# Projection units in seven products of quarters, beside a search for thresholds

## The chip, the cores and the metric

One NeuronCore of a Trainium2 chip runs the whole program. The time is the device time of one execution in microseconds; smaller is better. The kernel before was timed three times.

## The reference

The program is one inference step of a one-layer hybrid decoder: 1040 prompt rows (16 learned meta tokens and 1024 tokens) and 8 sequences of 8 new rows, 1104 rows of 1024 in all. Everything is float32. The normalised rows are multiplied by one wide matrix, and its columns are split:

```
h = rms_norm(x, norm1_g) @ w_in
p_r, p_a, g_r, g_a = split_cols(h)          # 1792, 1608, 1024, 1024 columns
y_r, s_fin, shift_last = rwkv7_branch(p_r, shift_prev, s_prev, lp)
q, k, v, qi, wi, ki = dsa_project(p_a, pos)
y_a = attend(q, k, v, qi, wi, ki)
merged = sigmoid(g_r) * (y_r @ w_br_rwkv) + sigmoid(g_a) * (y_a @ w_br_attn)
# in rwkv7_branch: prev = rows one step earlier
pm = p_r + (prev - p_r) * rwkv_mu
# in dsa_prompt, for each block of 128 queries:
score = sum_h relu(qi_h . ki) * wi_h;  keep the 256 highest visible keys;  softmax over them
```

The change touches only how `p_r`, `g_r` and `g_a` are multiplied for the prompt and new rows (the projection units), and when.

## The kernel before

The program runs in stages, each a block of five engine programs which ends when all engines have arrived. The stage of the change is `prompt_and_project` (from 223 to 876 us of the profile). `project_attention` stands before it and has left the normalised rows, turned, in `xT` (8 tiles of 128 channels by 1104 rows). `sample_scores` stands behind it.

`prompt_and_project` does two things at once: the sparse attention of the prompt, and 90 **projection units** that fill TensorE where the attention leaves it free. Unit `u` is tile `t = u // 3` of 128 output channels and column block `j = u % 3` of 368 rows (`COLS`). TensorE's `unit` (L437) is 8 products of 128 x 128 by 368, accumulated in one bank; a float32 product is two instructions in the profile. ScalarE's `evacuate` (L594 to L602) scales the bank into `PMT` and `PX` (tiles 0 to 13) or copies it into `PX` (the gates, tiles 14 to 29). For tiles 0 to 13 GpSimd adds the two (L685, 1040 wide, and L686) and SyncE stores the sum. SyncE loads the weights for two tiles at a time into one of two halves of `W`, as soon as the units of two loads earlier are done.

The stage goes through four parts:

1. The padding (`pad`, L788 to L801, VectorE) and the index products: TensorE `dot` (L453), ScalarE `rectify` (L614), VectorE `weigh` (L719, L721) sum up scores for 83 pieces. After every 20 pieces TensorE does a unit: units 0 to 3. The fifth piece waits for the padding.
2. The **search** (`bisect`): for each query VectorE finds the 256th highest score bit by bit, in 33 rounds. A round is seven counts over the scores (`tally`, L731 and L736, each a pass over up to 1024 columns), TensorE's `total` (L458), which adds up the part that is packed on partitions, a copy of it (L740), and three operations on 128 x 7 numbers (L755, L757, L760). TensorE has a fixed order: twelve product steps, one `total`, and so on (`SPACING` = 12), with units 4 to 58 (`AHEAD` = 59). The products for head team 0 (`scores(0)`) are issued before the search.
3. The choice (`choose`, VectorE), which turns scores into masks; its scan (L775) reads `ones`, set to 1 at the stage's start (L831).
4. 33 **teams** of heads, each two heads after the first. Per head: VectorE `peak_of` (L814), ScalarE `exponential` (L619), VectorE `normalise` (L825, L827), TensorE `tile_up` (L500), ScalarE `untile` (L633), and TensorE `values` (L516). The masks' width m falls from 1040 to 128 columns. `fills(x)` says in which teams a unit is done between these steps, half of it after each `tile_up`: before, in all teams but the last two.

GpSimd moreover issues two gathers of cached index keys (`gather_keys`, L277). The second one writes over `xT`, so it waits for the last projection unit. SyncE's wait for the last store and the drains of all engines end the stage (L366).

## Time and profile before

| | us |
|---|---|
| median of three runs | 2758.52 (2755.36 to 2760.3) |
| the profiled execution | 2736.69 |
| its span | 2734.9 |
| TensorE busy (PE) | 2589.1 (95%) |
| VectorE (DVE) | 1739.7 (64%) |
| ScalarE (ACT) | 788.5 (29%) |
| GpSimd (POOL) | 391.4 (14%) |

PE is the matrix engine's products and PEld its weight loads, which overlap them. Busy shares are means over stages with different limits, so the rows below are from stretches of the one stage. A row of a timeline is: start in us from the span's start, duration in us, engine, line of the program, operation, what it writes and reads, shapes, count, and in brackets how long the engine stood idle before it and what ended that. Several instructions in a row are merged; the duration is then from the first start to the last end. Mean granted clock of TensorE over the span: 0.965.

### The profile page before, as it was taken

Reading aid. Unit: us, or ns where it says so; the run is one execution under the profiler, and the core shown is the slowest. Engines: PE = TensorE matmul, PEld = TensorE weight load, DVE = VectorE, ACT = ScalarE, POOL = GpSimd, SP = SyncE. Lnnn points to the kernel's source line nnn. Section 1 sums busy time; section 2 is a strip of 40 time slices with the busy share of each in tenths; the row PEclk is TensorE's granted clock in tenths of the full one; section 3 lists DMA queues with packets and bytes.
Section 4 is the critical chain, followed back from the end, with each engine's and each line's share of the span. In section 5 each row is a group of like instructions: output and inputs, shape, how many; then the busy total and the mean of one; then the engine's idle time right before and its main releaser. Section 6 shows DMA issues by size and latency. Waiting matters only on the chain.

```text
span 2734.9 us, 49325 instructions
## 1 busy us (share of the span) xinstructions
PE 2589.1 (95%) x19336; PEld 1788.2 (65%) x19336; DVE 1739.7 (64%) x3313; ACT 788.5 (29%) x1725; POOL 391.4 (14%) x574
## 2 busy tenths in 40 slices
PE   8998999999997997898889999998999999999997
PEld 5553566666654323788756997655656666579997
DVE  3555888874533448666668999988762322357666
ACT  2224322124443653111112553012335321221212
POOL 0000111000000000000001663000335441011111
PEclk9999999999998986999999999999999999999999
DMA  8882112131113450000144664443337563533332
GB/s 297 308 292 86 41 64 88 65 103 37 49 41 106 178 162 27 4 27 12 66 146 160 234 241 167 133 122 129 106 133 242 180 201 117 173 124 123 124 124 72
DMA packets 95961, 348.79 MB, mean 128 GB/s; under 512 B 19561, under 2 KB 43977, under 8 KB 74033
## 3 DMA queue, kind: packets, MB, share of 16 engines
q1 hardware_dynamic: 83696, 294.50, 31.3%
q0 software_dynamic: 12032, 51.14, 5.8%
q8 instruction: 153, 2.51, 0.4%
q14 instruction: 80, 0.65, 0.1%
HBM read 289.57 MB, written 55.23 MB: 126 GB/s over the span
## 4 chain that ended last, share of the span: by engine, by line
PE 47%; DVE 7%; DVEq 3%; issue 1%; DMA 1%; POOL 0%; ACT 0%; POOLq 0%; ACTq 0%; SPq 0%
PE banks L2368 6%; PE banks L2281 5%; PE tl_P L2368 4%; PE banks L2313 4%; PE banks L2299 3%; PE tl_P L2313 3%; PE rc_P L1395 3%; PE banks L2213 3%; PE tl_P L2281 2%; DVE arena L2907 2%; DVEq L2905 2%; PE tl_P L2299 2%; DVE tl_v L2901 1%; PE tl_P L2213 1%; PE banks L1407 1%
## 5 line engine op out<-in xcount | busy, mean ns | idle before, releaser
L437 PE MATMUL dp_PS<-base,dp_W 128*128 128x368 f32 x1440 | 465.9, 476 | 0.0
L437 PEld LDWEIGHTS dp_PS<-base,dp_W 128*128 128x128 f32 x1440 | 265.8, 190 | 157.5 <-issue 8.8
L162 PE MATMUL pa_PG<-pa_W,base 128*128 128x402 f32 (+1 forms) x576 | 198.5, 504 | 7.8 <-DMA pa_W<-in_w_dsa 7.7
L736 DVE TENSOR_SCALAR_CACHE_REDUCE dp_EQ<-dp_SCORE,dp_trial 128x1024 f32<-128x1024 f32 (+1 forms) x186 | 176.0, 946 | 19.9 <-issue 0.9
L162 PEld LDWEIGHTS pa_PG<-pa_W,base 128*128 128x128 f32 (+1 forms) x576 | 106.7, 187 | 94.6 <-issue 14.2
L2281 PE MATMUL banks<-base,tl_WU 128*128 128x368 f32 x496 | 157.9, 475 | 0.8 <-DVE base L2960 0.8
L2299 PE MATMUL banks<-base,tl_WD 128*128 128x368 f32 x484 | 154.3, 474 | 0.0
L2901 DVE MAX8 tl_v<-arena 128x8 f32<-128x4100 f32 x32 | 141.8, 4431 | 3.4 <-issue 1.6
L2904 DVE FIND_INDEX8 tl_i<-tl_v,arena 128x8 uint32<-128x4100 f32 x32 | 141.5, 4423 | 0.0
L2907 DVE MATCH_REPLACE8 arena<-tl_v,arena 128x4100 f32<-128x4100 f32 x32 | 141.3, 4414 | 0.0
L2851 POOL DMA_INDIRECT arena<-in_cache_kv,tl_PHT x128 | 122.6, 958 | 109.9 <-PE tl_P L2447 73.8
L2281 PEld LDWEIGHTS banks<-base,tl_WU 128*128 128x128 f32 x496 | 94.0, 191 | 59.5 <-issue 2.8
L2299 PEld LDWEIGHTS banks<-base,tl_WD 128*128 128x128 f32 x484 | 90.5, 190 | 57.1 <-issue 3.7
L2553 ACT ACTIVATE arena<-base 128x368 f32<-128x368 f32 x44 | 22.1, 509 | 270.6 <-DVEq L2944 150.8
L814 DVE CUSTOM_DVE_ANT_0 dp_P<-dp_PS,dp_SCORE 128x1024 f32<-128x1024 f32 (+7 forms) x64 | 48.5, 758 | 66.7 <-PE dp_PS L487 58.8
L2313 PE MATMUL banks<-arena 128*128 128x184 f32 x504 | 85.6, 319 | 1.4 <-DVE arena L3075 1.4
L2225 PE MATMUL banks<-base,arena 128*128 128x368 f32 x256 | 81.3, 473 | 1.5 <-issue 1.1
L2313 PEld LDWEIGHTS banks<-arena 128*128 128x128 f32 x504 | 80.0, 190 | 1.6 <-issue 1.6
L2213 PE MATMUL banks<-arena 128*128 128x368 f32 x240 | 78.5, 480 | 1.1 <-DMA arena<-in_wb 1.1
L2281 PE MATMUL tl_P<-base,tl_WU 128*128 128x368 f32 x240 | 76.8, 473 | 0.0
L2520 POOL TENSOR_TENSOR base<-tl_T 128x368 f32<-128x368 f32 x36 | 30.6, 850 | 302.4 <-ACTq L2603 301.5
L594 ACT ACTIVATE dp_PMT<-dp_PS,dp_rest 128x368 f32<-128x368 f32 x42 | 23.8, 568 | 164.2 <-PE dp_PS L437 164.2
(525 smaller groups left out, 5077.1 us busy)
## 6 DMA issues: line engine op xcount, KB each, us to landing
tl_WU<-in_wu SPq DMA_DIRECT2D x58, 1024.0 KB, 4.9
pa_WQ<-in_wu SPq DMA_DIRECT2D x22, 1024.0 KB, 8.3
wsum<-pa_WS SPq DMA_DIRECT2D x22, 1024.0 KB, 4.9
tl_WD<-in_wd SPq DMA_DIRECT2D x32, 704.0 KB, 4.4
arena<-wsum SPq DMA_DIRECT2D x21, 1024.0 KB, 7.3
dp_W<-in_w_rw SPq DMA_DIRECT2D x15, 1024.0 KB, 5.5
arena<-in_wb SPq DMA_DIRECT2D x24, 512.0 KB, 3.8
arena<-in_wo SPq DMA_DIRECT2D x24, 512.0 KB, 3.8
```

Of the source, the lines that this page charges most:

```text
L162: last = pe.matmul(PG[0:n, c, 0:NC4], xT[:, k, r:r + n], W[:, c, k, :], start=k == 0, stop=k == KD - 1)
L437: last = pe.matmul(bank(f)[:, 0:w], W[:, t // 2 % 2, k, 128 * (t % 2):128 * (t % 2) + 128], xT[:, k, c:c + w], start=k == 0, stop=k == KD - 1)
L736: dve.tensor_scalar(EQ[0:n, 0:m], scored_of(j), values(n, x), None, op, ALU.add, accum_out=result[0:n, x:x + 1])
L2213: last = pe.matmul(out[:, 0:W], WM[:, i % 2, o:o + 128], YT[:, j, k, :], start=k == 0, stop=k == 3)
L2281: last = pe.matmul(out[:, 0:W], WU[:, i % 2, o:o + 128], XN[:, k, :], start=k == 0, stop=k == KD - 1)
L2299: last = pe.matmul(out[:, 0:W], WD[:, i % 3, 128 * e:128 * e + 128], HT[:, f, :], start=f == 0, stop=f == NF - 1)
L2313: last = pe.matmul(out[:, 0:H], weights[:, k, :], moving(k), start=first and k == 0, stop=k == 3, skip_group_check=True)
L2368: last = pe.matmul(out[:, 0:H], weights[:, k, :], moving(k), start=first and k == 0, stop=k == kk - 1, skip_group_check=True)
L2851: pool.indirect_dma_start(out=KV[:, n % 16, t, :], out_offset=None, in_=I["cache_kv"], in_offset=bass.IndirectOffsetOnAxis(ap=PHT[:, 64 * ...
L2901: dve.max(v8[:, :], SC)
L2904: dve.max_index(i8[:, :], v8[:, :], SC)
L2907: dve.match_replace(SC, v8[:, :], SC, TAKEN)
```

## The change

Two things change in `prompt_and_project`.

**Where the units are done.** `fills(x)` becomes true only for x < 27 of the 33 teams, so teams 27 to 30 lose their unit, and `AHEAD` becomes 63: four units more are done between the index products and the teams.

**How units 6 to 59 are done.** These are nine loads of weights (`PAIRS`, q = 1 to 9), each with three column blocks: 27 blocks (`NBL`), each of which makes two units at once, for two tiles of output channels and one column block. A block is a product of a 2 x 2 by a 2 x 2 matrix of quarters: input channels 0 to 511 and 512 to 1023, two output tiles, two halves of 184 rows (`H`). `seven` does it with seven products of quarters (each four TensorE products of 128 x 128 by 184) in place of eight, in banks 0 to 3, with partial results kept by ScalarE (`keep`, seven copies of 184 columns a block) and added by GpSimd (`f16`, `f167`, and three in `finish`). The products take sums of rows (`XF`, made once by `mix_rows` on GpSimd: two column blocks at the stage's start and the third after the index products) and sums of weights (`WF`, four sums of 512 columns for every load, on GpSimd: `weights_a`, `weights_b`, `weights_c`). The results are put together in `STG` in SBUF, from which `evacuate` reads them.

The row mixes of L685 and L686 become `mix_tile` and are called between these sums. `tick` keeps the distance of `total` at twelve steps, a half-width product counting a half. `scores(0)` is issued after the search, since it uses banks 0 to 2. The new tiles lie in the same memory as `RL`, `CUM`, `ones`, `P`, `PTS` and `YB` (one tensor `room_for`); hence `ones` is set after the search, once the evacuations up to unit 59 are done.

The core of the diff; the rest makes the waits and the numbering fit.

```
+    H = COLS[0][1] // 2
...
+        at[0] = 0
+        WF = cut(4 * 512).rearrange("p (i k m) -> p i k m", i=4, k=4)
+        f1, f6, f7, f16, f167 = (cut(H) for _ in range(5))
+        STG = cut(2 * 2 * H).rearrange("p (a n) -> p a n", a=2)
+        XF = cut(3 * 4 * 4 * H).rearrange("p (j i k n) -> p j i k n", j=3, i=4, k=4)
...
-            return int(m >= 256 or x < NTEAM - 2)
+            return int(m >= 256 and x < NTEAM - 6)
         AHEAD = NU - sum(fills(x) for x in range(NTEAM))
         fill_of = [AHEAD + sum(fills(y) for y in range(x)) for x in range(NTEAM)]
         bank = lambda f: PS[:, (4, 6)[f % 2]] if f < AHEAD else PS[:, 7]
+        PAIRS = range(1, AHEAD // 6)
+        BLOCKS = [(q, j) for q in PAIRS for j in range(3)]
+        NBL = len(BLOCKS)
+        by_seven = lambda u: u // 6 in PAIRS
+        nth_product = lambda u: u if u < 6 else u - 2 * NBL
+        nth_copy = lambda u: u // 6 * 6 + 2 * (u % 3) + u // 3 % 2 if by_seven(u) else u
+        FA, FB, FD, FE = (PS[:, x, 0:H] for x in range(4))
+        source = lambda u: STG[:, u // 3 % 2] if by_seven(u) else bank(u)
 
         def scores_of(u):
             m = size(u)[0]
...
                                          xT[:, k, c:c + w], start=k == 0, stop=k == KD - 1)
                     if end == KD:
                         last.then_inc(product, 1)
+
+                def seven(m, tick):
+                    q, j = BLOCKS[m - 1]
+                    c = COLS[j][0]
...
+
+                    def multiply(out, weights, e, moving, first, made):
+                        for k in range(4):
+                            last = pe.matmul(out, weights(e, k), moving(k), start=first and k == 0, stop=k == 3,
+                                             skip_group_check=True)
+                        last.then_inc(made, 1)
+                        tick(2)
+
+                    if j == 0:
+                        pe.wait_ge(w_in[q % 2], 16 * (q // 2 + 1))
+                    pe.wait_ge(fa_taken, 2 * m - 2)
+                    multiply(FA, raw, 0, left, True, fa_made)
+                    pe.wait_ge(xf_made, j + 1)
+                    pe.wait_ge(wf_made, 3 * q - 2)
+                    pe.wait_ge(fb_taken, 2 * m - 2)
+                    multiply(FB, mixed_w, 1, mix(1), True, fb_made)
+                    pe.wait_ge(fd_taken, 2 * m - 2)
+                    multiply(FD, mixed_w, 0, mix(0), True, fd_made)
+                    pe.wait_ge(fa_taken, 2 * m - 1)
+                    multiply(FA, raw, 1, low_left, False, fa_made)
+                    pe.wait_ge(wf_made, 3 * q - 1)
+                    pe.wait_ge(fb_taken, 2 * m - 1)
+                    multiply(FB, mixed_w, 2, mix(2), False, fb_made)
+                    pe.wait_ge(fe_taken, m - 1)
+                    multiply(FE, raw, 3, mix(3), True, fe_made)
+                    pe.wait_ge(wf_made, 3 * q)
+                    pe.wait_ge(fd_taken, 2 * m - 1)
+                    multiply(FD, mixed_w, 3, low_right, False, fd_made)
 
                 def dot(j, p):
...
+                pe.wait_ge(same_in, 16)
+                spent = [0, 0]
+
+                def tick(n):
+                    spent[0] += n
+                    if spent[0] >= SPACING * (spent[1] + 1) and spent[1] < ROUNDS:
+                        total(spent[1])
+                        spent[1] += 1
+
+                for f in range(AMONG, 6):
+                    for k in range(KD):
+                        unit(f, k, k + 1)
+                        tick(1)
+                for m in range(1, NBL + 1):
+                    seven(m, tick)
+                for f in range(6 * PAIRS.stop, AHEAD):
+                    for k in range(KD):
+                        unit(f, k, k + 1)
...
+                pe.wait_ge(fd_taken, 2 * NBL)
+                pe.wait_ge(fe_taken, NBL)
                 scores(0)
-                pe.wait_ge(same_in, 16)
-                steps = [(f, k) for f in range(AMONG, AHEAD) for k in range(KD)]
-                for i, (f, k) in enumerate(steps):
-                    unit(f, k, k + 1)
-                    if i % SPACING == SPACING - 1 and i // SPACING < ROUNDS:
-                        total(i // SPACING)
-                for r in range(len(steps) // SPACING, ROUNDS):
...
                             act.activation(seqs[:, :, 0], sh[:, t], ACT.Copy, scale=mu[:, t:t + 1])
-                    act.wait_ge(product, u + 1)
+                    if by_seven(u):
+                        act.wait_ge(f_done, (u // 6 - 1) * 3 + j + 1)
+                    else:
...
+                def keep(part, bank, made, taken, count):
+                    act.wait_ge(made, count)
+                    act.activation(part, bank, ACT.Copy).then_inc(taken, 1)
+
+                def both(m):
+                    q, j = BLOCKS[m - 1]
+                    act.drain()
+                    evacuate(6 * q + j)
+                    evacuate(6 * q + 3 + j)
+
+                def keep_block(m):
+                    if m > 1:
+                        act.wait_ge(f_mid, m - 1)
+                    else:
+                        act.wait_ge(weighted, len(all_pieces))
+                    keep(f1, FA, fa_made, fa_taken, 2 * m - 1)
+                    keep(f6, FB, fb_made, fb_taken, 2 * m - 1)
+                    if m > 1:
+                        both(m - 1)
+                    keep(STG[:, 1, H:2 * H], FD, fd_made, fd_taken, 2 * m - 1)
+                    keep(STG[:, 0, 0:H], FA, fa_made, fa_taken, 2 * m)
+                    keep(f7, FB, fb_made, fb_taken, 2 * m)
+                    keep(STG[:, 1, 0:H], FE, fe_made, fe_taken, m)
+                    keep(STG[:, 0, H:2 * H], FD, fd_made, fd_taken, 2 * m)
 
                 def rectify(j, p):
...
                     pool.memset(PX[:, i, 0:1], 0.0)
                 pool.drain().then_inc(zeroed, 1)
+
+                def mix_rows(j):
+                    c = COLS[j][0]
+                    high, low, to = xT[:, 0:4, c:c + 2 * H], xT[:, 4:8, c:c + 2 * H], XF[:, j]
+                    pool.tensor_tensor(to[:, 0], high[:, :, H:], high[:, :, 0:H], ALU.subtract)
+                    pool.tensor_tensor(to[:, 2], low[:, :, H:], high[:, :, H:], ALU.subtract)
+                    pool.drain()
+                    pool.tensor_tensor(to[:, 1], low[:, :, H:], to[:, 0], ALU.subtract)
+                    pool.drain()
+                    pool.tensor_tensor(to[:, 3], low[:, :, 0:H], to[:, 1], ALU.subtract)
+                    pool.drain().then_inc(xf_made, 1)
+
...
+                    pool.wait_ge(w_in[q % 2], 16 * (q // 2 + 1))
+                    pool.tensor_tensor(WF[:, 0], part_of(q, 2), part_of(q, 3), ALU.add)
+                    pool.drain()
+                    pool.tensor_tensor(WF[:, 1], WF[:, 0], part_of(q, 0), ALU.subtract)
+                    pool.drain().then_inc(wf_made, 1)
+
+                def weights_b(q):
+                    pool.tensor_tensor(WF[:, 2], part_of(q, 0), part_of(q, 2), ALU.subtract)
+                    pool.drain().then_inc(wf_made, 1)
+
+                def weights_c(q):
+                    pool.tensor_tensor(WF[:, 3], part_of(q, 1), WF[:, 1], ALU.subtract)
+                    pool.drain().then_inc(wf_made, 1)
+
+                def finish(m):
+                    pool.wait_ge(fd_taken, 2 * m)
+                    pool.wait_ge(fe_taken, m)
+                    pool.tensor_tensor(STG[:, 0, H:2 * H], STG[:, 0, H:2 * H], f16, ALU.add)
+                    pool.tensor_tensor(STG[:, 1, H:2 * H], STG[:, 1, H:2 * H], f167, ALU.add)
+                    pool.tensor_tensor(STG[:, 1, 0:H], STG[:, 1, 0:H], f167, ALU.add)
...
-                for t in range(NT):
-                    px, pm = PX[:, t % 2], PMT[:, t % 2]
-                    seqs = px[:, 1 + TP:].rearrange("p (b q) -> p b q", q=9)
-                    later_rows = pm[:, TP:R].rearrange("p (b q) -> p b q", q=8)
...
+                pool.wait_ge(weighted, len(all_pieces))
+                weights_a(PAIRS[0])
+                weights_b(PAIRS[0])
+                weights_c(PAIRS[0])
+                mix_tile(1)
+                mix_rows(2)
+                for m in range(1, NBL + 1):
+                    q, j = BLOCKS[m - 1]
+                    if m > 1:
+                        finish(m - 1)
+                        if j == 0:
+                            weights_c(q)
+                    pool.wait_ge(fa_taken, 2 * m - 1)
+                    pool.wait_ge(fb_taken, 2 * m - 1)
+                    pool.tensor_tensor(f16, f1, f6, ALU.add)
+                    if j == 0 and m > 1 and 2 * q - 2 < NT:
+                        mix_tile(2 * q - 2)
+                    if j == 2 and q + 1 in PAIRS:
+                        pool.wait_ge(fd_made, 2 * m - 1)
+                        weights_a(q + 1)
+                    pool.wait_ge(fb_taken, 2 * m)
+                    pool.tensor_tensor(f167, f1, f7, ALU.add)
+                    pool.drain().then_inc(f_mid, 1)
+                    if j == 0 and m > 1 and 2 * q - 1 < NT:
+                        mix_tile(2 * q - 1)
+                    if j == 2 and q + 1 in PAIRS:
+                        weights_b(q + 1)
+                finish(NBL)
...
-                pool.wait_ge(product, NU)
+                pool.wait_ge(product, NU - 2 * NBL)
...
                 dve.wait_ge(later_in, 16)
-                dve.memset(ones[:, :], 1.0)
                 pad()
...
                 bisect()
+                dve.wait_ge(copied, 6 * PAIRS.stop)
+                dve.memset(ones[:, :], 1.0)
+                dve.drain()
```

## Rows read from the trace of the kernel before

**Rows 1.** Windows: stretch, us, busy us per engine, PEclk, DMA, GB/s.
```profile
304.00:567.00 263.00, 262.80 (x890) 163.03 (x891) 225.57 (x598) 52.13 (x139) 32.11 (x26) 1.00 0.19 69
...
868.00:876.00 8.00, 0.33 (x4) 0.09 (x4) 0.00 (x0) 0.60 (x1) 0.00 (x0) 0.53 0.82 280
876.00:884.00 8.00, 3.41 (x33) 2.93 (x34) 3.14 (x14) 6.54 (x5) 1.02 (x2) 0.50 0.37 78
```

**Rows 2.** Timeline of the search's last rounds, TensorE and VectorE: start, us, engine.
```profile
545.33 0.38 PE L458 MATMUL dp_PS<-dp_part,dp_same 128*128 128x1 f32 x2
...
551.66 0.16 DVE L740 COPY dp_count<-dp_PS 128x1 f32<-128x1 f32 x1
...
559.42 0.16 DVE L740 COPY dp_count<-dp_PS 128x1 f32<-128x1 f32 x1
...
560.97 27.45 PE L437 MATMUL dp_PS<-base,dp_W 128*128 128x368 f32 x88
...
567.29 0.16 DVE L740 COPY dp_over<-dp_PS 128x1 f32<-128x1 f32 x1
```

**Rows 3.** Timeline of the search's entry and first round, VectorE.
```profile
305.86 0.92 DVE L844 COPY base<-base 64x128 f32<-64x128 f32 x4
...
307.36 0.29 DVE L731 TENSOR_SCALAR_CACHE_REDUCE dp_EQ<-dp_PACK 128x130 f32<-128x130 f32 x1
...
315.63 0.16 DVE L740 COPY dp_count<-dp_PS 128x1 f32<-128x1 f32 x1 [1.99 <-PE dp_PS L458]
```

**Rows 4.** Timeline of TensorE in a later stage: two blocks of seven half-width products.
```profile
1525.80 1.49 PE L2313 MATMUL tl_P<-base,tl_WU 128*128 128x184 f32 x8
...
1534.60 1.41 PE L2313 MATMUL tl_P<-base,tl_WU 128*128 128x184 f32 x8
```

**Rows 5.** Groups by form, GpSimd: line, op, tiles, shapes, count, busy, mean ns.
```profile
L685 POOL TENSOR_TENSOR dp_PMT<-dp_PMT,dp_PX 128x1040 f32<-128x1040 f32 x14 | 31.0, 2217 | 211.3 <-ACTq L603 211.3
...
L2801 POOL TENSOR_TENSOR base<-arena 128x184 f32<-128x184 f32 x21 | 12.1, 576 | 0.0
...
L2030 POOL TENSOR_TENSOR arena<-tl_WU 128x512 f32<-128x512 f32 x1 | 1.3, 1265 | 117.2 <-DMA tl_WU<-in_wu 117.2
```

**Rows 6.** Timeline and one line's instructions: VectorE beside a GpSimd instruction.
```profile
503.06 2.03 POOL L685 TENSOR_TENSOR dp_PMT<-dp_PMT,dp_PX 128x1040 f32<-128x1040 f32 x1 [12.62 <-ACTq L603]
503.13 1.98 DVE L755 TENSOR_SCALAR dp_step<-dp_count 128x7 int32<-128x7 f32 x1
...
1540.87 0.45 DVE L2908 COPY arena<-tl_v 128x8 f32<-128x8 f32 x1
...
L755 DVE TENSOR_SCALAR dp_step<-dp_count x31: 170/171/1983, 323.5 to 559.7; 128x7 int32<-128x7 f32 x31
...
L731 DVE TENSOR_SCALAR_CACHE_REDUCE dp_EQ<-dp_PACK,dp_trial x31: 348/348/351, 316.4 to 552.6; 128x130 f32<-128x130 f32 x31
```

**Rows 7.** Timeline of the stage's start: GpSimd, VectorE, TensorE.
```profile
223.68 0.13 POOL L675 MEMSET dp_PX<- 128x1 f32 x2 [38.49 <-POOLq L37]
...
230.01 0.93 DVE L831 MEMSET dp_ones<- 128x1040 f32 x1 [7.32 <-DMA dp_later<-in_later]
...
232.92 0.28 PE L536 MATMUL dp_PS<-ident,dp_WD 16*128 16x16 f32 x1 [5.68 <-DVEq L805]
```

**Rows 8.** Timeline of the last teams, TensorE and VectorE.
```profile
836.96 0.66 PE L516 MATMUL dp_PS<-dp_PTS,V 128*64 128x128 f32 x8
...
866.31 0.44 PE L516 MATMUL dp_PS<-dp_PTS,V 128*64 128x128 f32 x4 [1.91 <-ACTq L637]
...
861.04 0.29 DVE L814 CUSTOM_DVE_ANT_0 dp_P<-dp_PS,dp_SCORE 128x128 f32<-128x128 f32 x1 [4.02 <-PE dp_PS L487]
...
863.26 0.29 DVE L827 TENSOR_SCALAR dp_P<-dp_P,dp_den 128x128 f32<-128x128 f32 x1
```

**Rows 9.** Instructions of L366, the end of the stage's block: min/median/max ns, start.
```profile
L366 POOLq DRAIN  x1: 11388/11388/11388, 863.7 to 863.7; - x1
...
L366 SPq DRAIN  x1: 7/7/7, 870.0 to 870.0; - x1
```

More of the change, by code:

```diff
@@ L369, in load @@
                 def load(p):
-                    if p >= 2:
-                        sp.wait_ge(product, 6 * (p - 1))
+                    if p - 2 in PAIRS:
+                        sp.wait_ge(fd_made, 6 * (p - 2))
+                    elif p >= 2:
+                        sp.wait_ge(product, nth_product(6 * (p - 2)) + 6)
                     sp.dma_start(W[:, p % 2], I["w_rw"][:, p]).then_inc(w_in[p % 2], 16)
@@ L378, in sends @@
                     if j == 2 and t >= NT:
[L379 removed]
+                        sp.wait_ge(copied, nth_copy(u) + 1)
                         sp.dma_start(gates[t - NT], PX[:, t % 2, 0:R]).then_inc(gate_out[t % 2], 16)
@@ L433, in unit @@
                     if first == 0 and f >= 2:
-                        pe.wait_ge(copied, f - 1 if f < AHEAD else f)
+                        past = f if f >= AHEAD else f - 1 if not by_seven(f - 2) else 6
+                        pe.wait_ge(copied, past)
                     c, w = COLS[j]
@@ L542, in _ @@
                 pe.wait_ge(rectified, len(all_pieces))
[L543 to L551 removed]
+                pe.wait_ge(same_in, 16)
[14 more added lines that the diff above has]
+                        unit(f, k, k + 1)
+                        tick(1)
+                for r in range(spent[1], ROUNDS):
+                    total(r)
+                pe.wait_ge(fa_taken, 2 * NBL)
+                pe.wait_ge(fb_taken, 2 * NBL)
+                pe.wait_ge(fd_taken, 2 * NBL)
+                pe.wait_ge(fe_taken, NBL)
+                scores(0)
                 pe.wait_ge(copied, AHEAD)
@@ L654, in _ @@
                         evacuate(d // EVERY)
-                for f in range(AMONG, AHEAD):
+                for f in range(AMONG, 6):
+                    evacuate(f)
+                for m in range(1, NBL + 1):
+                    keep_block(m)
+                both(NBL)
+                for f in range(6 * PAIRS.stop, AHEAD):
                     evacuate(f)
@@ new lines, in weights_c @@
+                def weights_c(q):
[7 more added lines that the diff above has]
+                    pool.tensor_tensor(STG[:, 1, 0:H], STG[:, 1, 0:H], f167, ALU.add)
+                    pool.drain().then_inc(f_done, 1)
@@ new lines, in mix_tile @@
+                def mix_tile(t):
+                    px, pm = PX[:, t % 2], PMT[:, t % 2]
+                    seqs = px[:, 1 + TP:].rearrange("p (b q) -> p b q", q=9)
+                    later_rows = pm[:, TP:R].rearrange("p (b q) -> p b q", q=8)
+                    pool.wait_ge(copied, nth_copy(3 * t + 2) + 1)
+                    pool.tensor_tensor(pm[:, 0:TP], pm[:, 0:TP], px[:, 0:TP], ALU.add)
+                    pool.tensor_tensor(later_rows, later_rows, seqs[:, :, 0:8], ALU.add)
+                    pool.drain().then_inc(mixed, 1)
@@ L677, in _ @@
+                mix_rows(0)
+                mix_rows(1)
                 pool.wait_ge(weighted, dots0[0] + len(pieces(0)) + 1)
@@ L679, in _ @@
                     pool.dma_start(PACK[16 * x:16 * x + 16, :], SCORE[0:16, PW16 * x:PW16 * x + PW16]).then_inc(packed, 16)
-                for t in range(NT):
-                    px, pm = PX[:, t % 2], PMT[:, t % 2]
-                    seqs = px[:, 1 + TP:].rearrange("p (b q) -> p b q", q=9)
-                    later_rows = pm[:, TP:R].rearrange("p (b q) -> p b q", q=8)
-                    pool.wait_ge(copied, 3 * t + 3)
-                    pool.tensor_tensor(pm[:, 0:TP], pm[:, 0:TP], px[:, 0:TP], ALU.add)
-                    pool.tensor_tensor(later_rows, later_rows, seqs[:, :, 0:8], ALU.add)
-                    pool.drain().then_inc(mixed, 1)
+                mix_tile(0)
+                pool.wait_ge(weighted, len(all_pieces))
[4 more added lines that the diff above has]
+                mix_rows(2)
+                for m in range(1, NBL + 1):
+                    q, j = BLOCKS[m - 1]
[19 more added lines that the diff above has]
+                finish(NBL)
                 pool.wait_ge(masked, 1)
```

35 lines of the change are left out of this document (25 added, 10 removed).

## Prediction

> **What bounds the kernel now.** I read the windows first, to find which engines are full in the stage that changes. In the search (304 to 567 us) TensorE is busy for 262.8 of 263 us and VectorE for 225.6, GpSimd for 32.1 [rows 1]. A full TensorE suggests that cheaper products would pay, so the next view is the timeline of one round. One round's `count` is read at 551.66 and the next one's at 559.42: 7.76 us, with VectorE waiting for nothing, while TensorE's twelve product steps (24 instructions, at 27.45/88 = 0.312 us each) take 7.49 us [rows 2]. The search has two full engines; VectorE sets its end (567.29), and TensorE's 88 leftover instructions (27.45 us) run beside the choices that follow [rows 2]. The teams of heads after it are bound by TensorE as long as a unit of products is filled into each. At the end of the block SyncE is ready at 870.0, but GpSimd's drain, which began at 863.7, lasts 11.39 us [rows 9], and 8 us pass with TensorE empty [rows 1].
>
> **TensorE in the search.** Before: 55 units of 8 products; 88 instructions are 5.5 units, so 5.0 us a unit, 275 us. After: units 4 and 5 and 60 to 62, 25 us, and 27 blocks of seven half-width products. Such a block takes 8.80 us in the later stage (1525.80 to 1534.60) [rows 4] instead of two units' 10.0, so 27 blocks are 238 us. Together 263 us: TensorE does four units more in 12 us less. But as VectorE sets the end, those 12 us are worth nothing; what counts is what the sums on GpSimd do to VectorE.
>
> **GpSimd beside VectorE.** L755, a 128x7 operation on VectorE, starts at 503.13, just after GpSimd's L685 (503.06, 2.03 us), and takes 1.98 us where the middle one of 31 takes 0.17; a 128x8 copy in a later stage takes 0.45 us in the same way. The tallies do not mind: all 31 of L731 take 348 to 351 ns [rows 6]. Each round has three such small operations (L755, L757, L760) between its last tally and the next. GpSimd's instructions are 0.58 us (184 wide), 1.27 (512) and 2.22 (1040) [rows 5]. In the search it will have 27 x 5 of 184, 9 x 4 of 512, four of 736 (between 512 and 1040: about 1.6 us, an estimate), and 13 row mixes of 1040 (2.22, and 0.3 allowed for L686): 78 + 46 + 6 + 33 = 163 us of some 285, busy 57%. An operation that arrives at random waits on average the sum of the squared durations over twice the time: (135 x 0.33 + 36 x 1.61 + 4 x 2.6 + 13 x 4.9) / 570 = 0.31 us. The second and third come 0.25 us later; GpSimd's instructions stand mostly in rows of two or three, so the next one has often begun: 0.2 us each. That is 0.7 us a round and 22 us in 32 rounds, less the 1.8 us that L755 lost before: **+20.6 us**. Bounds: only one wait a round, +8; three waits of about 0.45, +40.
>
> The Trainium skill (SBUF — State Buffer, section "Who interferes with whom") says that whoever issues first holds the shared port pair for its whole instruction while the other fully blocks, and that on VectorE this concerns two-port modes and two inputs from SBUF. The row for L755 agrees (1.98 us against 0.17). By that rule all three small operations are exposed, which gives the 20.6; by the row alone only L755 is, which gives the lower bound of +8.
>
> **The start of the stage.** Eight 736-wide sums (`mix_rows` 0 and 1) now start on GpSimd at 223.7 and last until about 236.6. VectorE's padding had its 0.93 us memset of `ones` at 230.01 [rows 7] and then six small copies and a sum (L793 to L801). The memset leaves (-0.9), but each of those seven operations now lets one GpSimd instruction pass, so the padding ends at about 238, not 232.9, when TensorE had waited 5.68 us for it [rows 7]. TensorE is nearly full from there to the search, so all passes on: **+5.0** (bounds -0.9, if copies slip in between, and +6).
>
> **Entry of the search.** GpSimd's first four weight sums (4 x 1.27 = 5.1 us) start as VectorE does its last causal add, the index, four copies of L844 and one more before its first tally at 307.36 [rows 3]: **+3.8** (+1.3 to +5.3). The first tally waited 1.99 us for TensorE [rows 3] behind `scores(0)`, which is moved behind the search: **-1.9**. The memset comes back between search and choice, with drain **+1.0**; its wait for 60 evacuations is met by then, since the last block ends a round before. `scores(0)` and the three leftover units (13.7 us) are done before VectorE's three choices are.
>
> **TensorE's clock.** TensorE then has nothing to do for about 12 us until the first peak. After the 8 us with no product the granted clock was 0.50 for the next 8 us [rows 1]. At 1.2 instead of 2.4 GHz the first full microseconds cost about half of themselves: **+2.5** (0 to +5).
>
> **Last teams.** From the values of team 26 to those of team 31 it took 836.96 to 866.31 = 29.35 us [rows 8], four of the five intervals holding a unit of 5.0. Without it VectorE's own work is 861.04 to 863.55 = 2.5 us, and its 4.02 us wait for score products held a half unit of 2.5, so 1.5 remains [rows 8]: 4.0 us a team, four of them and the 2.7 of the last: 18.7, so -10.6. As TensorE is then under half busy its clock may fall here too, +1.6: **-9** (-15 to -5).
>
> **End of the block.** The second gather waits for the last product, which now comes about 18 us before the end of the block instead of 5; the drain's 11.4 us fit in. SyncE's 870.0 then sets it, not 875.1 [rows 9]: **-5** (0 to -5).
>
> Every step's waits in `seven` have cover: the sums of block m-1 (1.75 us), ScalarE's two evacuations (about 2.5 us) and one copy end before the seventh product of block m, 7.5 us in; if that cover goes, each microsecond is paid 27 times. SyncE's weight load still waits for the block two ahead; the row mixes' DMAs come at most 2 us later.
>
> **Sum.** +5.0 + 3.8 - 1.9 + 20.6 + 1.0 + 2.5 - 9 - 5 = **+17 us**. The profiled execution took 2736.69 us (span 2734.9), so 2754; the median of the timed runs is 2758.52, 22 us above, and the prediction goes with it: 2775.5 us.
>
> **Rivals.** (A) The forecast, VectorE slowed by GpSimd, chance 0.55.
> (B) Faster: the small operations rarely meet a GpSimd instruction, because GpSimd's instructions follow TensorE's products in a fixed order while the tallies' ends fall in between. Then -1.9 - 0.9 + 1 + 2.5 - 9 - 5 = -13 us: 2745. For it: in the whole search only one of 31 L755 was caught, with GpSimd busy 12%. Against: 57% busy, and a block has 14 steps and a round 12, so their phases drift through all positions. It decides when a round loses less than 0.15 us. Chance 0.16.
> (C) One wait a round (+8 for +20.6) and the padding untouched: about -1 to +4, 2760. Chance 0.12.
> (D) GpSimd itself becomes the bound: waits for VectorE and ScalarE stretch its chain beyond 9.5 us a block, TensorE waits in `seven`, and the tallies come late. At 10.5 us a block 27 blocks take 284 us, and three waits a round, together +35 to +40: 2796. For it: 6 us of GpSimd a block and in a block with two row mixes 9. Against: no row shows it falling behind. Chance 0.17.
>
> **Range and chances.** 0.2% is 5.5 us, about what a measurement of this kernel can tell from none. Slower by more: A and D and a little of C, 0.74; within: the rest of C, 0.10; faster: B, 0.16. The range takes in B's near end and nearly all of D: 2745 to 2796; A's own is 2763 to 2790.
>
> **What would show it.** The distance of L740's copies: 8.3 to 8.7 us (7.76 kills A, and 9.5 or more speaks for D). L755, L757 and L760 with durations above 0.2 us, each ending with a GpSimd instruction. TensorE's wait for `padded` ending near 238. Last interval of values 4.0 us instead of 6.7. L366's drain on GpSimd over before SyncE's, and the next stage 1 us after it. If TensorE waits for `xf_made`, `wf_made` or a `taken` inside the blocks by more than 1 us each, the chain that I took as covered was not.

## The result and the profile after

The changed kernel took 2765.12 us (median of 11 runs, 2757.44 to 2770.13) against 2755.36 for the kernel before (11 runs): ratio 1.0031, 95% interval [1.0017, 1.0045]. By this ratio it is slower by 8.5 us (the two medians lie 9.8 us apart); the forecast was +17. The time lies inside the forecast's range of 2745 to 2796 us, but only half of the forecast change came.

The first comparison of profiles misleads. The profiled execution of before took 2736.69 us, less than each of its timed runs (2751 and more); the one of the changed kernel took 2757.44. Cut at the ends of the stages, the 20 us do not stand where the code differs. The last of the rows below is SyncE's release at the end of the stage of the change, the counterpart of 875.3 before (870.0 plus the rest of GpSimd's drain [rows 9]); L389 is L366 before.

```profile
L389 POOLq DRAIN  x1: 10546/10546/10546, 857.1 to 857.1; - x1
...
L389 SPq DRAIN  x1: 7/7/7, 878.6 to 878.6; - x1
...
L389 SPq EVENT_SEMAPHORE  x1: 17/17/17, 878.8 to 878.8; - x1
```

The stage ends 3.5 us later than before. Three stages on, at 1395.5 (before 1396.0), even that is gone in this pair of profiles; the last stage, whose code is the same, takes 1358.9 us instead of 1337.7. TensorE's timeline of the changed kernel there shows where:

```profile
2070.67 0.77 PE L2466 MATMUL banks<-base,tl_WU 128*128 128x368 f32 x1 [2.33 <-issue]
2073.47 0.77 PE L2466 MATMUL banks<-base,tl_WU 128*128 128x368 f32 x1 [2.03 <-issue]
2076.27 0.77 PE L2466 MATMUL banks<-base,tl_WU 128*128 128x368 f32 x1 [2.03 <-issue]
```

One product, then 2 us in which TensorE waits for nothing that the profile shows, again and again, while GpSimd issues its gathers. The experiments start with this stretch, since a price of 20 us would have hidden all others.

The windows of the changed kernel, for the same length of the search, for the choices behind it, and for the first team's start (columns as in [rows 1]):

```profile
322.00:585.00 263.00, 253.32 (x1579) 245.22 (x1577) 229.67 (x574) 113.19 (x326) 152.99 (x197) 0.99 0.23 75
594.00:609.00 15.00, 2.72 (x12) 1.44 (x10) 13.66 (x15) 0.16 (x1) 5.35 (x9) 0.66 0.78 214
609.00:617.00 8.00, 7.73 (x27) 4.01 (x28) 3.70 (x8) 2.56 (x5) 0.00 (x0) 0.78 0.00 0
```

GpSimd is busy for 153 us of 263 instead of 32, TensorE for 253 instead of 263: its twelve product steps are over before VectorE's round is. The three small operations of a round, the read of the total, and the tallies (lines' instructions; min/median/max in ns):

```profile
L938 DVE TENSOR_SCALAR dp_step<-dp_count x31: 170/173/1495, 329.5 to 577.7; 128x7 int32<-128x7 f32 x31
L940 DVE TENSOR_TENSOR dp_bits<-dp_bits,dp_step x31: 166/167/529, 329.9 to 577.9; 128x7 int32<-128x7 int32 x31
L943 DVE TENSOR_SCALAR dp_trial<-dp_bits x30: 170/171/1882, 330.1 to 570.4; 128x7 int32<-128x7 int32 x30
L923 DVE COPY dp_count<-dp_PS x32: 157/159/160, 321.6 to 577.4; 128x1 f32<-128x1 f32 x32
L919 DVE TENSOR_SCALAR_CACHE_REDUCE dp_EQ<-dp_SCORE,dp_trial x186: 612/946/1281, 323.0 to 576.7; 128x1024 f32<-128x1024 f32 x31, 128x896 f32<-128x896 f32 x31, 128x768 f32<-128x768 f32 x31, 128x640 f32<-128x640 f32 x31
```

The medians are untouched. A stretched operation starts inside a GpSimd instruction and ends 0.02 to 0.03 us after one; the longest, on VectorE and GpSimd:

```profile
386.65 1.88 DVE L943 TENSOR_SCALAR dp_trial<-dp_bits 128x7 int32<-128x7 int32 x1
386.48 2.02 POOL L833 TENSOR_TENSOR dp_PMT<-dp_PMT,dp_PX 128x1040 f32<-128x1040 f32 x1 [0.18 <-issue]
```

Of the 92 small operations 30 last longer than 0.2 us: 5.4, 2.4 and 6.4 us too much for the three lines. 31 rounds take 255.8 us (321.6 to 577.4; before 243.8 [rows 2, 3]). Start of the stage and entry of the search, VectorE and TensorE:

```profile
229.68 3.36 DVE L976 COPY dp_QZ<-QT 64x32 f32<-64x32 f32 x4
233.35 1.59 DVE L983 COPY dp_QIZ<-base 64x64 f32<-64x64 f32 x2
234.96 1.75 DVE L984 TENSOR_TENSOR dp_WD<-ident,WI 16x128 f32<-16x128 f32 x1
...
309.23 1.40 DVE L884 SCALAR_TENSOR_TENSOR dp_SCORE<-dp_later,dp_SCORE 128x128 f32<-128x128 f32 x1
310.71 1.21 DVE L1022 TENSOR_SCALAR idx<-pt,base 128x8 int32<-128x8 int32 x1
311.83 1.89 DVE L1026 COPY base<-base 64x128 f32<-64x128 f32 x4
313.74 1.17 DVE L1028 COPY base<-KIT 128x64 f32<-128x64 f32 x1
...
315.27 0.29 DVE L914 TENSOR_SCALAR_CACHE_REDUCE dp_EQ<-dp_PACK 128x130 f32<-128x130 f32 x1
```

```profile
236.79 0.28 PE L600 MATMUL dp_PS<-ident,dp_WD 16*128 16x16 f32 x1 [9.63 <-DVEq L988]
...
608.95 3.72 PE L551 MATMUL dp_PS<-base,QT 64*128 64x512 f32 x8 [12.28 <-DVEq L1002]
...
856.98 0.66 PE L580 MATMUL dp_PS<-dp_room_for,V 128*64 128x128 f32 x8
...
874.25 0.70 PE L580 MATMUL dp_PS<-dp_room_for,V 128*64 128x128 f32 x4 [0.45 <-ACTq L746]
```

The padding ends at 236.8 instead of 232.9 [rows 7], the first tally starts at 315.3 instead of 307.4 [rows 3], and TensorE stands idle for 12.28 us before the second team's scores. The last two rows answer to 836.96 and 866.31 of [rows 8]: 17.3 us instead of 29.35.

### The profile page after: what moved, and what is told of

Read it like the earlier page. It is cut to its first block, busy times and chain, and to the rows that moved or that the text cites. A ratio compares the mean times of both kernels' runs of the same rounds, so it can differ in the third digit from the quotient of the medians.

```text
span 2755.6 us, 51292 instructions
## 1 busy us (share of the span) xinstructions
PE 2571.3 (93%) x19984; PEld 1862.5 (68%) x19984; DVE 1761.6 (64%) x3313; ACT 849.2 (31%) x1914; POOL 531.9 (19%) x757
## 4 chain that ended last, share of the span: by engine, by line
PE 47%; DVE 7%; DVEq 3%; issue 1%; another core or an unknown queue 1%; DMA 1%; ACT 0%; POOL 0%; ACTq 0%; SPq 0%; POOLq 0%
PE banks L2553 6%; PE banks L2466 5%; PE tl_P L2553 4%; PE banks L2498 4%; PE banks L2484 3%; PE tl_P L2498 3%; PE tl_P L2466 3%; PE banks L2398 3%; PE rc_P L1580 2%; DVE arena L3092 2%; DVE tl_v L3086 2%; DVEq L3090 2%; PE tl_P L2484 2%; PE tl_P L2398 1%; PE banks L1592 1%
## 5 line engine op out<-in xcount | busy, mean ns | idle before, releaser
L463 PE MATMUL dp_PS<-base,dp_W 128*128 128x368 f32 x576 | 190.0, 476 | 1.0 <-ACT dp_room_for L723 1.0
L162 PEld LDWEIGHTS pa_PG<-pa_W,base 128*128 128x128 f32 (+1 forms) x576 | 106.7, 187 | 94.5 <-issue 14.2
L463 PEld LDWEIGHTS dp_PS<-base,dp_W 128*128 128x128 f32 x576 | 104.7, 190 | 64.6 <-issue 8.8
L480 PE MATMUL dp_PS<-dp_room_for 128*128 128x184 f32 x648 | 111.7, 321 | 0.0
L480 PEld LDWEIGHTS dp_PS<-dp_room_for 128*128 128x128 f32 x648 | 102.4, 190 | 0.0
L691 ACT ACTIVATE dp_room_for<-dp_PS 128x184 f32<-128x184 f32 x189 | 57.5, 324 | 126.5 <-PE dp_PS L480 120.7
L997 DVE CUSTOM_DVE_ANT_0 dp_room_for<-dp_PS,dp_SCORE 128x1024 f32<-128x1024 f32 (+7 forms) x64 | 48.5, 758 | 57.7 <-PE dp_PS L551 50.3
```

The lines of the kernel that those rows point to most:

```text
L162: last = pe.matmul(PG[0:n, c, 0:NC4], xT[:, k, r:r + n], W[:, c, k, :], start=k == 0, stop=k == KD - 1)
L463: last = pe.matmul(bank(f)[:, 0:w], W[:, t // 2 % 2, k, 128 * (t % 2):128 * (t % 2) + 128], xT[:, k, c:c + w], start=k == 0, stop=k == KD - 1)
L480: last = pe.matmul(out, weights(e, k), moving(k), start=first and k == 0, stop=k == 3, skip_group_check=True)
```

## The experiments

In the expectations T1 is what I took for true, R (R1, R2, R3) a rival. Each kernel was timed beside the kernel before on the same chip, in four groups. In them before took 2755, 2736, 2756 and 2735 us (the last two groups carry the same chip number); so ratios are given, and the ends of the stage, which did not depend on that.

**A second profile of each kernel** (b0: before; a0: changed; no edit).

> The kernel before, unchanged, for a second profile. In the profiles at hand the stage of the change ends 3.5 us later after the change (875.3 to 878.8), the stage behind the two next ones takes it back (312.9 to 309.0 us), and the whole difference of 20.7 us stands in the last stage (1337.7 to 1358.9 us), whose code is the same: between 2063 and 2087 TensorE waits about 2.03 us ahead of one product after another, put down to issue. T1: this stretch is chance (the first profile of before was an execution without it, 2736.7 us against 2751 to 2762 in eleven timed ones): then this profile has it too, in an execution of 2750 to 2762 us with 1350 to 1360 us in the last stage. R1: the stretch belongs to the changed kernel: then the last stage is 1338 +- 3 here again and the execution about 2737.

> The changed kernel, unchanged, for a second profile. All theories: the stage of the change ends at 878.8 +- 1.5, the mean round of the search is 8.2 to 8.3 us. T1: the last stage differs from its 1358.9 by up to 20 us either way. R1: it is 1359 +- 3.

b0 took 2753.97 us, and its last stage 1358.5; a0 2757.47, with 1357.3. TensorE's rows of the kernel before (b0) in the same place:

```profile
2069.42 0.77 PE L2281 MATMUL banks<-base,tl_WU 128*128 128x368 f32 x1 [1.33 <-issue]
2072.22 0.77 PE L2281 MATMUL banks<-base,tl_WU 128*128 128x368 f32 x1 [2.03 <-issue]
2075.02 0.77 PE L2281 MATMUL banks<-base,tl_WU 128*128 128x368 f32 x1 [2.03 <-issue]
```

R1 falls: the stretch belongs to neither kernel. In all profiles of my runs beside which before took 2755 us the last stage lasts 1357 to 1361 us, beside 2736 us 1333 to 1341, whatever the kernel; only the first profile of before (1337.7, beside timed runs of 2755) doesn't fit this. Stage ends: before 875.3 and 874.3, changed 878.8 and 879.4. The stage costs 3.5 to 5.1 us, not 17. Three stages on, this second pair still stands 4.7 us apart (1392.4 and 1397.1), so that the difference was gone there in the first pair was chance.

**Half of the change each** (fills_only: before with the new `fills`; seven_only: changed with the old).

```
-            return int(m >= 256 or x < NTEAM - 2)      # before -> fills_only
+            return int(m >= 256 and x < NTEAM - 6)     # after -> seven_only: the reverse
```

> The kernel before with fills(x) as in the change (four units moved from teams 27 to 30 to before the teams) and all else left. T1 (the terms of the prediction): the rounds stay 7.86 us on average, the four units follow the search on a full TensorE (+20), the last teams give back 9 to 10.6, and the drain at the end of the block is hidden (-5): stage end at 880 to 882, time +4 to +7 us, ratio about 1.002. R2: the last teams are bound by TensorE without their unit too: then it gives all 20 back, and the stage ends at 870 to 872.

> The changed kernel with fills(x) of before (units in all but the last two teams, AHEAD = 59; 24 blocks of seven instead of 27, units 54 to 58 by eight products). T1: the start (+5 to 6) and the rounds (mean 8.2 to 8.3 us) are as in the changed kernel, the last teams take 6.7 us each again (+9 to +10), and GpSimd's drain at the end of the block is late again (+5): stage end 892 to 895, 14 to 16 us later than the changed kernel, ratio to before about 1.007. R2 (it is the fills that cost, and seven products are free): stage end at 875 +- 2.

fills_only: stage end 875.4, ratio 1.0013 [1.0001, 1.0025]. seven_only: stage end 896.3, ratio 1.0068 [1.0049, 1.0088]. R2 falls both times. T1 was 5 us too high for fills_only: the first team came 18 us later and the last teams gave 13 back, not 10. It was 1 us too low for seven_only. Without seven products the four units cost 1 us in the profile and 3.6 us in the timed runs; beside seven products they are worth 17 us (896.3 against 879; seven_only also has 24 blocks of seven instead of 27, since `AHEAD` is 59). They fill idle time: in seven_only TensorE waits twice as long before the second team's scores (its waits: us in total, times, longest), and the stage ends 4.4 us after SyncE's drain, with GpSimd's.

```profile
PE dp_PS L551 <- DVEq L1002: 24.3, 1, 24.3
```

**Row sums after the padding** (late_rows).

```
+                pool.wait_ge(padded, 1)
                 mix_rows(0)
                 mix_rows(1)
```

> The changed kernel, but GpSimd waits for VectorE's padding before the row sums of the first two column blocks. T1 (the small copies of the padding queue behind GpSimd's 736-wide sums): TensorE's wait for the padding is 5.0 us again (9.5 in the changed kernel), and the stage ends 4 us earlier, at 874.5 to 876; GpSimd's sums now meet the weighting of the first pieces, which costs 1 us or none. R2: they set that chain back by as much as they did the padding: stage end 878.5 to 880.

T1 and R2 both had the sign wrong: stage end 888.0, ratio 1.0036 [1.0024, 1.0048]. The padding is as quick as before (0.54 us for the four copies that took 3.36), but the weighting is not. Timelines of VectorE and GpSimd:

```profile
230.21 0.54 DVE L977 COPY dp_QZ<-QT 64x32 f32<-64x32 f32 x4
...
234.01 8.46 DVE L905 SCALAR_TENSOR_TENSOR dp_SCORE<-dp_room_for,WI,dp_SCORE 128x512 f32<-128x512 f32 x4
242.88 6.03 DVE L905 SCALAR_TENSOR_TENSOR dp_SCORE<-dp_room_for,WI,dp_SCORE 128x512 f32<-128x512 f32 x3
```

```profile
241.88 2.20 POOL L796 TENSOR_TENSOR dp_room_for<-base 128x736 f32<-128x736 f32 x1
244.22 2.00 POOL L798 TENSOR_TENSOR dp_room_for<-base,dp_room_for 128x736 f32<-128x736 f32 x1
```

VectorE's back-to-back sums of two SBUF inputs take turns with GpSimd's, 2.1 us each instead of 0.84 (3.36 for four in a0): 8.6 us lost in these seven. Beside that TensorE does 26 instructions from 240 to 260 where it did 61 in a0, at a granted clock of 0.57 (a0: 0.99), and VectorE then waits 7.9 us for TensorE's L531 where it waited 3.65 in a0; what of this is the clock's share no run separates. The padding was the cheaper victim.

**Two more units ahead** (more_ahead: `x < NTEAM - 8`), **numbers of the search in PSUM** (psum_state), and these with late_rows (combined).

```
+                    count, b_ps = PS[:, 7, 0:NS], PS[:, 7, 8:8 + NS].bitcast(I32)   # psum_state
-                        dve.tensor_tensor(bits[:, :], bits[:, :], step[:, :], ALU.bitwise_xor)
+                        dve.tensor_tensor(b_ps if b else bits[:, :], b_ps, step[:, :], ALU.bitwise_xor)
...
+                            dve.tensor_scalar(trial[:, :], b_ps, 1 << (b - 1), None, ALU.bitwise_xor)
```

> The changed kernel with two units more moved ahead of the teams (fills for x < NTEAM - 8, AHEAD = 65; still 27 blocks of seven). TensorE stands idle for 12.3 us before the first peak of the changed kernel, and two units are 10 us. T1: the peak comes at the same time (+-0.5 us), teams 25 and 26 take 2.2 to 2.7 us less each, and the idle time that lowered TensorE's clock is gone (-0.5 to -1): stage end at 873 to 875. R2 (more of the last teams are bound by a chain of VectorE and ScalarE, which the unit only fills): stage end 878 to 879.

> The changed kernel with count and bits of the search held in a bank of PSUM, so that each of the three small operations of a round has an input from PSUM instead of SBUF. In the changed kernel 28 to 33 of the 92 last longer than 0.2 us, 14.2 and 15.1 us in all (two profiles). T1 (they wait for GpSimd at a port of SBUF that a source in PSUM does not need): none of them is above 0.35 us, the rounds lose at most 0.1 us each for access to PSUM, mean 7.80 to 7.95 instead of 8.23, stage end 866 to 871, unless TensorE's blocks now set the rounds, for which 7.6 us each is enough. R3 (it is any access to SBUF, or the output, that waits): a third or so still stretched, mean round above 8.15.

> All three edits together: row sums after the padding, two more units ahead, count and bits in PSUM. T1: their gains add up, except that the search now ends 12 us earlier relative to TensorE, so the two units and the three leftover ones (24 us) are no longer hidden in full behind the choices: 4 + 12 + 5 less 2 to 4. Stage end at 860 to 864, 11 to 15 us before the kernel before, ratio 0.994 to 0.997. If the parts overlap (R): ratio 0.999 to 1.001.

more_ahead: stage end 876.7, ratio 1.0001 [0.9992, 1.0010], 2 us later than T1. The teams give 5.5 us back as expected; the rounds happened to lose 17.6 us to GpSimd instead of 14 to 15, which took half of it. psum_state: 876.9, 1.0006 [0.9996, 1.0016]. Its lines:

```profile
L939 DVE TENSOR_SCALAR dp_step<-dp_PS x31: 165/165/166, 330.8 to 575.7; 128x7 int32<-128x7 f32 x31
L941 DVE TENSOR_TENSOR dp_PS<-dp_PS,dp_step x30: 173/174/174, 331.0 to 567.8; 128x7 int32<-128x7 int32 x30
L944 DVE TENSOR_SCALAR dp_trial<-dp_PS x30: 166/166/167, 331.3 to 568.1; 128x7 int32<-128x7 int32 x30
L919 DVE DVE_READ_ACCUMULATOR dp_EQ<-dp_SCORE,dp_trial x186: 140/142/144, 325.1 to 575.2; 128x1 f32 x186
```

This is the cleanest evidence for the mechanism: with one input in PSUM no small operation is stretched by a nanosecond, beside the same sums on GpSimd. Most of the gain was lost again, since the six accumulators a round that are now read into PSUM take 0.142 instead of 0.083 us, 11 us in 32 rounds; the median round is 8.12 us, and T1's stage end (866 to 871) was missed. combined: 879.1, 1.0013 [1.0004, 1.0022], neither T1 nor R; late_rows' loss of 9 us goes through it and takes what the two others gave.

**Only what is needed** (bits_only: `bits` in PSUM, `count` in SBUF; weights_later; two_edits: both; three_edits: `mix_rows(1)` moved as well; "mean round" is over 32 rounds).

```
-                pool.wait_ge(weighted, len(all_pieces))    # weights_later
+                pool.wait_ge(indexed, 1)
                 weights_a(PAIRS[0])
...
-                mix_tile(1)                                # three_edits; out of the stage's start
+                mix_rows(1)
+                mix_tile(1)
```

> The changed kernel with only bits in PSUM. With count and bits there no small operation was stretched, but each of the seven READ_ACCUMULATOR of a round took 0.14 instead of 0.08 us and the mean round was 8.13. T1 (an operation that reads or writes two things in SBUF at the double rate, or reads two, waits for GpSimd): L938's successor (count to step, both in SBUF) is still stretched in a third of the rounds, 4 to 6 us in all, the two others never; mean round 7.90 to 8.00, stage end at 869 to 872 against 879. R3 (only the accumulators' detour held the small operations out of GpSimd's way in time): the two others are stretched again, mean round above 8.1.

> The changed kernel, but GpSimd's first four weight sums wait for VectorE's index and query copies (indexed) instead of the last weighting. T1: the operations ahead of the search (1.39, 1.21, 1.89 and 1.16 us in the changed kernel, 0.29, 0.23, 0.92 and 0.19 before) are as before, the first tally starts 4 us earlier (311.2 against 315.2), TensorE still finds the sums made at its first block; stage end 875 to 876. R2: the sums come too late and TensorE's first block and so the rounds start 2 to 4 us later: stage end 878 to 879.

> The two edits together (bits in PSUM, first weight sums after the copies). T1: the search ends 12 to 14 us earlier than in the changed kernel; TensorE then has no idle time before the first peak, and its own work (594 to 597 us until the scores of the first team) begins to set it: stage end 866 to 869, 6 to 9 us before the kernel before (874.3, 875.3), ratio 0.997 +- 0.0015. If the gain is lost to TensorE altogether: stage end 873 or later, ratio 1.000.

> The same, and the row sums of the second column block moved from the stage's start to behind the first weight sums. T1: the padding meets at most one GpSimd sum more (230 to 231 us), TensorE's wait for it is 6 to 7 us instead of 9.5, 2.5 to 3.5 us gained at the first tally; of these 1 to 2 are lost where the sums for the second block come late. Stage end 864 to 868. R: GpSimd's queue in the first three blocks gets so long (it now carries 14 us of row sums there) that TensorE waits 5 us or more: stage end 870 or later, later than two_edits.

| | first count | mean round | lost in small operations | stage end | ratio |
|---|---|---|---|---|---|
| bits_only | 321.9 | 7.97 | 5.6 | 870.5 | 0.9990 [0.9982, 0.9999] |
| weights_later | 318.3 | 8.41 | 20.1 | 881.2 | 1.0025 [1.0015, 1.0034] |
| two_edits | 318.1 | 8.05 | 8.4 | 869.6 | 0.9980 [0.9966, 0.9994] |
| three_edits | 312.9 | 8.22 | 7.4 | 869.9 | 0.9982 [0.9972, 0.9992] |

bits_only, two of its three lines:

```profile
L939 DVE TENSOR_SCALAR dp_step<-dp_count x31: 170/171/1260, 329.7 to 569.6; 128x7 int32<-128x7 f32 x31
L944 DVE TENSOR_SCALAR dp_trial<-dp_PS x30: 165/166/167, 330.4 to 562.3; 128x7 int32<-128x7 int32 x30
```

T1 holds to the line: the operation with both ends in SBUF is still caught, the one with a source in PSUM is not. weights_later removes the 1.40, 1.21, 1.89 and 1.17 us (VectorE's first tally at 311.95 instead of 315.27) and is not faster than the changed kernel by its stage end (881.2): shifted by 3 us, the rounds lose 20.1 instead of 15 to the same GpSimd sums, met at other places. Both T1 and R2 were too early here. With `bits` out of reach (two_edits) most of that lottery is gone, but not the part of `count`. The search ends 9 to 10 us earlier than in the changed kernel, not 12 to 14, and my guess that TensorE would then set the start of the teams was wrong: it still waits 12.3 us before the scores. In three_edits the rival came true by its cause: GpSimd has all row sums of the second and third column block to do before the first sum of block 1 (`f16`, at 329.47); ScalarE waits 7.8 us for it, TensorE 4.7 us for ScalarE, and VectorE for TensorE's total, twice, 6.6 us in all. The longer of the two:

```profile
340.61 0.16 DVE L923 COPY dp_count<-dp_PS 128x1 f32<-128x1 f32 x1 [4.01 <-PE dp_PS L522]
```

**Controls and the best version.** before_bits is the kernel before with bits_only's edit, two_ahead and three_ahead are two_edits and three_edits with `x < NTEAM - 8`, after_again is the changed kernel.

> The kernel BEFORE with bits of the search in PSUM. GpSimd is nearly idle there (13% busy in the search), so by T1 the edit finds nothing to save but the one stretched operation (1.65 to 1.8 us): mean round 7.80 to 7.86, stage end 872.5 to 875, ratio 0.9995 to 1.0000. If the 0.999 of bits_only comes from a cheaper round as such (R), the rounds here are shorter than 7.76 in the median and the ratio is 0.997.

> two_edits with two units more ahead of the teams (x < NTEAM - 8). two_edits still shows TensorE idle for 12.3 us before the first peak. T1: the peak is not moved, teams 24 and 25 give 5.4 us back: stage end 864 +- 1, ratio 0.996 to 0.997. R: TensorE's two units end behind the peak: stage end 867 or later, ratio 0.998.

> three_edits with the same two units more ahead. TensorE's idle time before the first peak was 10.3 us there. T1: stage end 864 to 865. R: 868 or later. Against two_ahead: no difference that can be told, since three_edits and two_edits differed by 0.3 us in stage end.

> The changed kernel again, timed beside the others of this call. Two profiles ended its stage 4 to 5 us later than before (878.8 and 879.4; 875.3 and 874.3), the timed runs gave +8.5 us [1.0017, 1.0045]. T1: stage end 879 +- 1 in this profile too, ratio 1.001 to 1.003, as the stage alone gives 0.0018; if it is 1.003 or more again, timed runs lose 3 us or more outside of what the profiles show.

before_bits: stage end 874.4, ratio 1.0003 [0.9994, 1.0012]. The edit is worth nothing that can be told where GpSimd is nearly idle (its one stretched operation, from `count`, stays), so the 8 to 9 us that it gains in bits_only are those of the contention. two_ahead: stage end 864.2, ratio 0.9966 [0.9954, 0.9978], faster than both kernels by a third of a per cent and more; TensorE's wait before the scores has shrunk as it should:

```profile
570.53 23.74 PE L463 MATMUL dp_PS<-base,dp_W 128*128 128x368 f32 x76
594.11 3.95 PE L542 MATMUL dp_PS<-base,dp_QZ 128*128 128x512 f32 x12
600.43 2.55 PE L551 MATMUL dp_PS<-base,QT 64*128 64x512 f32 x8 [2.37 <-DVEq L1003]
```

three_ahead: 863.8, 0.9972 [0.9963, 0.9981], as good. after_again: stage end 880.0, ratio 1.0032 [1.0021, 1.0042].

## Why the prediction was wrong

The direction and the mechanism held, the size was off by half: +17 us forecast, +8.5 measured. The step that failed is the term for GpSimd beside VectorE: +20.6 us forecast, 12.4 to 13.4 measured. All terms, from the two profiles of each kernel (stage ends +3.5 and +5.1):

- **TensorE in the search.** Right in what it was worth: the products of units 4 to 62 take 271 us of TensorE instead of 280 (forecast 263 instead of 275), and the saving brought nothing, since VectorE sets the end.
- **GpSimd beside VectorE, the step that failed.** +20.6 forecast; measured 14.2 (15.2 in a0, 15.2 in after_again) less 1.8, so 12.4 to 13.4. The mean round was 8.23 to 8.26 us, where 8.3 to 8.7 had been named as the sign. GpSimd's busy time was right (160 us from 304 to 585; 163 forecast). What was too high is the price per operation. I charged the mean wait of a random arrival to the first of the three (0.31 us) and 0.2 to each other, as if an operation paid its whole wait. In the profile of the changed kernel 16, 9 and 10 operations of the three lines start inside a GpSimd instruction, with 7.2, 3.7 and 7.8 us still to run, 18.7 in all where the forecast had 22; the second starts inside one in 9 of 31 rounds, not in most. And of the 18.7 only 5.4, 2.4 and 6.4 us are lost: an operation that is alone for 0.17 us ends 0.02 to 0.03 us after the GpSimd instruction, so 0.10 to 0.15 us of its own time lie within the wait. About 3.5 of the 8 us too many are fewer and shorter meetings, 4.5 this overlap. The forecast's own range (+8 to +40) held this; its middle did not.
- That term is a throw of dice as well. Against one and the same load it came out at 14.2 us (the changed kernel, first count read at 321.6), 17.6 (more_ahead, 322.2) and 20.1 (weights_later, 318.3). A sum over phases gives a mean; one kernel is one draw, and that this one was low is in part luck.
- **Start and entry.** Padding +5.0 forecast, +3.9 measured; entry +3.8 forecast, +4.0 measured (5.67 us for four groups of operations against 1.6); the first round's wait -1.9, as forecast. late_rows and weights_later show both causes.
- **`ones` and the clock.** +1.0 forecast, +1.2 measured between the last count and the next scores. TensorE's idle time was forecast as about 12 us and is 12.28. I priced it only by the clock (+2.5 forecast; the granted clock was 0.66 and 0.78 in the windows around it, and the teams' first values came 1.4 us later still). I did not see it as what it was, a reserve for two more units worth 5.4 us: two_ahead spent it.
- **Last teams.** -9 forecast, -12.1 measured (29.35 to 17.3 us). The interval of the last three fell to 3.6 to 4.2 us, near the forecast 4.0; but the first two after the last unit took 3.1 and 2.5, for their peaks (847.5 and 854.4) lay ahead of it, beside the units. The clock did fall, as allowed for: it was granted at 0.50 from 862 to 876, where it was 1.00 before, and four score products took 0.80 us instead of 0.49; the 17.3 us hold this.
- **End of the block.** -5 forecast, -5.1 measured: GpSimd's drain (10.5 us) starts at 857.1 and is over when SyncE arrives. seven_only, with its units back in the last teams, waits for it again.

For the first pair these terms add up to +3.8, where the stage's end moved by +3.5. So the stage was overrated by 12 to 13.5 us: 7 to 8 in the contention, 3 in the last teams, 1 each in the padding and the clock. The time differs by less, since the timed runs lost 8.5 us where the stage shows 3.5 to 5. after_again gave the same 1.0032 beside a stage end of 880.0. In the thirteen other kernels the timed difference and that of the stage (against 874.7, the mean of before, b0 and before_bits) lie up to 3.4 us apart, either way, so 4 is hardly out of the ordinary, and the lower end of the interval is 4.7 us; but it came back in both timings. Where the changed kernel loses it, if it does, stays open.

Of the rivals, C (one wait a round, time about 2760) came nearest by its number, but not by its reason: the padding was hit. B fell at the 30 stretched operations. D fell since VectorE never waited for TensorE in the search: inside the blocks five products waited for ScalarE's copies, 5.3 us in all. One of these waits, of 2.1 us, is longer than the 1 us that had been named as the sign against the cover; it did not reach VectorE. (The upper end of A's own range, 2790, is not its bound of +40 carried through, which gives 2795.)

The Trainium skill (SBUF — State Buffer, section "Who interferes with whom") says that on VectorE the shared port pair is needed for two-port modes and for two inputs from SBUF. The runs agree in both directions: the one-input operation from bits to trial (L943) was stretched to 1.88 us with its source in SBUF and stayed at 0.166 with its source in PSUM. The tallies kept their 0.61 to 1.28 us beside the same sums.

## What to carry to other kernels

Before moving sums to GpSimd, list the small VectorE operations on the path beside it: here each with both ends, or two inputs, in SBUF lasted now and then until the end of a GpSimd instruction, up to 1.9 us. Moving one operand of them to PSUM freed them at 0.01 us or less, as long as no accumulator was read into PSUM for it. When a faster engine goes idle ahead of a slower one, look for work from a stretch that this engine bounds, and move exactly the idle time's worth of it. And before reading a difference of two profiles, cut both at the ends of the stages: here 21.2 us stood in a stage whose code had not changed.

## What the runs showed that I had not expected

- The same last stage takes 1333 to 1341 us in some profiles and 1357 to 1361 in others, for every kernel tried. It is not the chip alone: with one and the same chip number the third group of runs had the long stage and the fourth the short one. In the long one TensorE gets a product only every 1.4 to 2.8 us for some 17 us while GpSimd issues gathers; the profile names no releaser, and no run settles the cause.
- A weighting sum of 128 x 512 (two SBUF inputs, 0.84 us alone) takes 2.1 us while GpSimd's 736-wide sums run back to back, and these slow too, from 1.75 to 2.0 or 2.2 us.
- Reading an accumulator into PSUM took 0.142 us, into SBUF 0.083.
